# The transposed delta-rule inverse in a hybrid decoder block: 32x32 block transposes on VectorE in place of TensorE turns and ScalarE copies

## What is computed

```python
a_mat = jnp.where(strict, jnp.einsum("bhnid,bhnjd->bhnij", kb, kc) * decay, 0.0)
rhs = jnp.concatenate([vb, kb * jnp.exp(gcum)[..., None]], axis=-1)
sol = lax.linalg.triangular_solve(a_mat + jnp.eye(c, dtype=f32), rhs, left_side=True,
                                  lower=True, unit_diagonal=True)
value, kcd = sol[..., :dv], sol[..., dv:]
```

## Time and profile before

| | |
|---|---|
| median of 3 runs | 565.91 us |
| lowest and highest run | 564.29 and 566.18 us |
| span of the profiled execution | 562.4 us |
| TensorE busy | 556.3 us (99%) |
| VectorE busy | 386.9 us (69%) |
| ScalarE busy | 309.4 us (55%) |
| GpSimd busy | 73.0 us (13%) |
| DMA, mean | 175 GB/s |

### The profile page before, as it was taken

The page is one execution under the profiler, slowest core; times in us unless marked ns, Lnnn a source line. Parts: engine busy times, 40 slices in busy tenths (PEclk is TensorE's granted clock), DMA queues, the critical chain, the costliest instruction groups (busy, mean ns, idle before and its releaser), DMA issues.

```text
span 562.4 us, 9437 instructions
## 1 busy us (share of the span) xinstructions
PE 556.3 (99%) x3695; PEld 482.1 (86%) x3695; DVE 386.9 (69%) x618; ACT 309.4 (55%) x530; POOL 73.0 (13%) x90
## 2 busy tenths in 40 slices
PE   8999999999999999999999999999999999999997
PEld 8999999787787898888888888898888888888885
DVE  6879988858375735898874575666666666757564
ACT  6767668626455656665745434466555545454541
POOL 4221211872610000035000000000000000000000
PEclk9999999999999999999999999999999999999999
DMA  9945576275995461344252556654657666566622
GB/s 300 261 146 175 179 189 225 83 228 198 239 230 178 152 224 32 120 150 147 91 203 84 177 198 196 178 152 151 212 167 217 171 204 194 180 185 191 202 98 75
DMA packets 95323, 98.14 MB, mean 175 GB/s; under 512 B 4986, under 2 KB 75661, under 8 KB 95280
## 3 DMA queue, kind: packets, MB, share of 16 engines
q1 hardware_dynamic: 92992, 93.63, 53.0%
q0 software_dynamic: 2000, 2.87, 2.7%
q10 hardware_dynamic: 288, 1.05, 0.5%
HBM read 96.39 MB, written 1.84 MB: 175 GB/s over the span
## 4 chain that ended last, share of the span: by engine, by line
PE 95%; DVE 3%; ACT 1%; DMA 1%; issue 0%; DVEq 0%; ACTq 0%
PE ps L1537 19%; PE ps L1539 18%; PE ps L1538 18%; PE ps L1653 14%; PE ps L1656 7%; PE ps L1542 4%; PE ps L1776 4%; PE ps L1939 2%; PE ps L1913 2%; PE ps L1628 1%; PE ps L1802 1%; PE ps L1811 1%; DMA x_sb<-in_x 1%; PE ps L1936 1%; DVE out_sb L1530 0%; DVE w_lo L1038 0%
## 5 line engine op out<-in xcount | busy, mean ns | idle before, releaser
L1038 DVE TENSOR_TENSOR w_lo<-raw,w_hi 128x2048 fp32r<-128x2048 f32 x74 | 171.5, 2317 | 96.8 <-ACT w_hi L653 96.7
L653 ACT ACTIVATE w_hi<-raw 128x2048 fp32r<-128x2048 f32 x74 | 141.6, 1913 | 80.5 <-PE ps L1539 71.1
L1653 PE MATMUL ps<-h_both,w_hi 128*128 128x512 f32 x352 | 122.4, 396 | 0.2 <-issue 0.2
L1656 PE MATMUL ps<-h_both,w_lo 128*128 128x256 f32 x352 | 91.1, 279 | 0.3 <-DVE h_both L1064 0.3
L1653 PEld LDWEIGHTS ps<-h_both,w_hi 128*128 128x128 f32 x352 | 63.8, 188 | 13.7 <-issue 2.0
L1656 PEld LDWEIGHTS ps<-h_both,w_lo 128*128 128x128 f32 x352 | 66.3, 188 | 4.0 <-issue 0.6
L1537 PE MATMUL ps<-w_hi,h_both 128*128 128x512 f32 x160 | 65.4, 409 | 0.3 <-DVE zs L1392 0.2
L1539 PE MATMUL ps<-w_hi,h_both 128*128 128x512 f32 x160 | 62.6, 391 | 0.0
L1538 PE MATMUL ps<-w_lo,h_both 128*128 128x512 f32 x160 | 62.4, 390 | 0.0
L1537 PE MATMUL ps<-h_both,w_hi 128*128 128x256 f32 x208 | 59.5, 286 | 0.0
L1538 PE MATMUL ps<-h_both,w_hi 128*128 128x256 f32 x208 | 58.8, 283 | 0.0
(11 more groups left out here) (391 smaller groups left out, 969.3 us busy)
## 6 DMA issues: line engine op xcount, KB each, us to landing
raw<-in_w_in SPq DMA_DIRECT2D x29, 1024.0 KB, 5.1
raw<-in_w_gate SPq DMA_DIRECT2D x22, 512.0 KB, 3.9
raw<-in_w_up SPq DMA_DIRECT2D x22, 512.0 KB, 5.1
raw<-in_w_down SPq DMA_DIRECT2D x11, 1024.0 KB, 4.8
raw<-in_cmp_w SPq DMA_DIRECT2D x8, 1024.0 KB, 5.7
raw<-in_w_proj_a SPq DMA_DIRECT2D x4, 1024.0 KB, 4.9
raw<-in_w_proj_b SPq DMA_DIRECT2D x4, 1024.0 KB, 5.1
raw<-in_w_out SPq DMA_DIRECT2D x4, 1024.0 KB, 5.0
```

Of the source, the lines that this page charges most:

```text
L653: nc.scalar.activation(w_hi[s % NSPL][:], raw[RAW_OF[n]][:], ACT.Copy).then_inc(hi_done, 1)
L1038: nc.vector.tensor_tensor(w_lo[s % NSPL][:], raw[RAW_OF[n]][:], w_hi[s % NSPL][:].bitcast(f32), ALU.subtract).then_inc(lo_done, 1)
L1653: cross = lambda stop: pe.matmul(banks[part][:], hi[:, k, part * P:(part + 1) * P], h_both[:, :, k, :], start=(k == 0), stop=stop)
L1656: end = pe.matmul(banks[part][:, 0:SEQ], lo[:, k, part * P:(part + 1) * P], h_hi[:, k, :], start=False, stop=False)
```

## The change

The stages `T4` and `T5` are taken out of the list of stages, with their places, their TensorE transposes and their ScalarE copies. In their place VectorE transposes blocks of 32x32 elements directly from `Db` into `DTb`, right after its part of `Y4` and `Y5`. After level 4 the four 32x32 diagonal blocks have changed, and four instructions move them; after level 5 the blocks in rows 32 to 63 and 96 to 127 beside them have changed, and two instructions move these. Each instruction has 32 partitions by 16 problems by 32 columns. The new semaphore `inverse_turned` is raised by the last of them; `Y5` waits for its first step, `Z6` for its second.

```diff
-    STAGES += [f"X{_l}"] + ([f"Y{_l}", f"T{_l}"] if _l < LEVELS - 1 else [f"Z{_l}"])
+    STAGES += [f"X{_l}", f"Y{_l}" if _l < LEVELS - 1 else f"Z{_l}"]
...
-            ("cmpv", 0, 0): "X4", ("wv", 0, 0): "Y4", ("wv", 0, 1): "T4", ("cmpv", 1, 0): "X5", ("wv", 1, 0): "Y5", ("wv", 1, 1): "T5",
+            ("cmpv", 0, 0): "X4", ("wv", 0, 0): "Y4", ("cmpv", 1, 0): "X5", ("wv", 1, 0): "Y5",
...
-                    if name == "knT" or name[0] in "XT":
-                        dst = {"k": ATb, "X": AXb, "T": DTb}[name[0]]
+                    if name == "knT" or name[0] == "X":
+                        dst = ATb if name == "knT" else AXb
...
+            def turn_inverse(l):
+
+                for b in range(NB - GRING, NB):
+                    wait_use(dve, f"Y{l}", b)
+                s = 32
+                if l == FIRST_LEVEL:
+                    moves = [(i, i) for i in range(P // s)]
+                else:
+                    moves = [(i + 1, i) for i in range(0, P // s, 2)]
+                for i, o in moves:
+                    ins = nc.vector.transpose(DTb[o * s:o * s + s, :, i * s:i * s + s], Db[i * s:i * s + s, :, o * s:o * s + s])
+                ins.then_inc(inverse_turned, 1)
...
                     for name, blocks in slot_stages(n, half):
                         gdn(name, blocks)
+                        if name[0] == "Y":
+                            turn_inverse(int(name[1:]))
...
-                        if name[0] == "T":
-                            src, before = Db, f"Y{name[1:]}"
...
                         if l > FIRST_LEVEL:
-                            wait_use(pe, f"T{l - 1}", b)
+                            pe.wait_ge(inverse_turned, l - FIRST_LEVEL)
```

More of the change, by code:

```diff
@@ L369, in hybrid_block @@
             "sub_out", "sub_in", "solved", "sub_back", "diag_in"))
+        inverse_turned = sem("inverse_turned")
         small_raw, small_mm = sem("small_raw"), sem("small_mm")
@@ L1780, in gdn @@
                             last = transpose(b4[:, q, :], p4(kT if name == "kt" else vT)[:, q, :])
-                    elif name == "knT" or name[0] == "T":
-                        if name[0] == "T":
-                            src, before = Db, f"Y{name[1:]}"
-                        else:
-                            src, before = AXb, "kt"
-                        wait_use(pe, before, b)
+                    elif name == "knT":
+                        wait_use(pe, "kt", b)
                         for q in range(4):
-                            last = transpose(b4[:, q, :], p4(src)[:, q, :])
+                            last = transpose(b4[:, q, :], p4(AXb)[:, q, :])
                     elif name in ("gram", "kq"):
```

## The result

| | before | changed |
|---|---|---|
| median, us (4 runs each, same chip) | 565.38 | 568.92 |
| lowest and highest, us | 564.29 to 566.18 | 568.41 to 569.36 |
| span of the profiled execution, us | 562.4 | 566.4 |
| granted clock, mean of an execution | 1.00 | 0.997, 0.994, 0.994, 0.994 |

The ratio is 1.0069, 95% interval 1.0053 to 1.0084: slower by 3.5 us by the medians, clear of 0.3%. On another chip the ratio was 1.0065 (1.0052 to 1.0078). No measurable change (566.4 us) had been forecast as the likeliest, at 0.64, and 0.31 given to slower; 568.92 lies just inside the range.

The account below looks back on a forecast made before the run. TensorE was taken to bound the kernel. A wait at the first place (+2.1) and a gain at the second (-1.67) summed to +0.45 us on the 562.4 us span, giving 566.4 us, range 564.8 to 569.0.

Parts of the forecast that it names:

- What bounds the kernel: Whole kernel: TensorE, busy 99% of the span and 95% of the last chain, so work taken from its queue shortens it.
- the 1.78 and 1.77 us on TensorE: At `T4` and `T5`: time of the removed TensorE transposes, 3.55 us gained if nothing else moved.
- The ScalarE copies: Eight copies into `DTb`, 2.07 us for four, go too; counted at nothing.
- The missing cover: `wv` 0: `keys(0)` queues behind four transposes, so TensorE waits some 3.8 us for `key_n`; +2.1 us.
- Rival B: Behind the new 3.8 us stall the clock falls to half rate, adding 1.5 to 3 us; about 568.2 us, chance 0.17.
- the likeliest case: Whole kernel: no measurable change, 566.4 us, second place's gain eaten up by the first's wait; chance 0.60.
- the sum (+0.45): Both places together: +2.1 - 1.67 = +0.45 us on a span of 562.4, so 562.85.
- The second place: `wv` 1, level 5 transposes: TensorE 1.77 us earlier, no wait, 0.1 allowed for what is tight; -1.67 us.
- A: VectorE transposes at the price of scattered operands, 1.08 us row: +2.65, 568.5 us, slower; chance 0.15.
- C: Full saving at both places, `key_n` not late: 3.55 us gained, 562.4 us; chance 0.04.
- D: VectorE's work hidden at both places and TensorE not on the path: time stays at 565.9 us; chance 0.04.
- the lower end: VectorE transpose price from a 512-element MEMSET, 0.48 us: 1.7 us for the four of level 4.

Follow-up runs that it names:

- level 5 only: Against the kernel before: only `T5` goes to two VectorE transposes, `T4` stays on TensorE with its ScalarE copies; 562.70 us, ratio 0.9960.
- the kernel with `keys(0)` first: Against the changed kernel: on VectorE `keys(0)` runs right behind `Y4`, the four level 4 transposes behind it; 563.23 us, 0.9970 of the kernel before.
- the filled kernel: Against the changed kernel: 20 identity matmuls on TensorE ahead of its wait for `key_n`; 566.56 us, 1.0027 of the kernel before.
- the two covered kernels: Against the changed kernel: transposes and `key_tok` turn moved where nothing should wait, 562.97 us (0.9979); then also the query norms' root ahead of `Y4`, 564.79 us (0.9993).

## Why the prediction was wrong

- **What bounds the kernel, and the 1.78 and 1.77 us on TensorE.** Right: `Y5` to the turn of `sc` is 1.78 us shorter, and level 5 only gains 2.2 us. The ScalarE copies cost and gave nothing.
- **The missing cover.** Right in kind: the wait stands at `key_tok`, and the order on VectorE makes it, as the kernel with `keys(0)` first shows. It was undersized: +2.87 us for +2.1. The transposes took 2.85 us for the 2.49 of the nearest row, and began 0.13 behind the last `copy_predicated`, not 0.03; no overlap with the next instruction came back (the sum took off 0.1); and TensorE started 0.15 behind the end of the scaling (170.48 to 170.63), not 0.05.
- **The clock.** This is the step that failed. Rival B described what happened, at its place and with its price (568.2 us), and was given 0.17; the likeliest case had a stall of 3.8 us and no fall. The reason given against it, that no row shows a fall, was no reason: the longest wait in those rows was 1.0 us, so they could not show what one of 3.8 us does. With a wait of 3.8 us the clock falls in 10 runs of 11. With the fall in the likeliest case the forecast would have been rival B's 568.2; measured was +1.57 us for the one fall in the profiled execution. The rule cited beside it, from the Trainium skill (TensorE: Matmul & The Clock Gate, Why this matters for your kernels), that idle gaps between bursts bring the lower clock back, held: behind the 4.5 us the granted clock is 0.50. It is the term that decides between no change and slower: the filled kernel, with the same wait and the clock kept, stands at 1.0027, just within the 0.3% that the prediction called no change. It is not the whole miss. Of the 3.55 us between the sum (+0.45) and the profiled span (+4.0), the clock is 1.57, the longer wait 0.74, `Z6` 0.3, and 0.97 lie outside both places. So that 568.2 comes within 0.7 us of 568.92 is in part luck: rival B too had the shorter wait and nothing for the 0.97.
- **The second place.** Right but for `Z6`: +0.40 us instead of 0.1. The end of the split came at 186.95, against 185.3 for the end of `TURN_LC`, and the logits behind it were later by more than the chain's slack. That the transposes ahead of them did it is shown by the kernel in which they stand behind the logits, where the distance is 8.61 us again.
- **Not in the sum at all:** +0.14 ahead of `Y4` and +0.83 behind the turn of `pc`. The former is within the scatter between executions: `Y4` starts anywhere from 160.2 to 161.4 us in the sixteen traces, with the same matmuls ahead of it. 0.35 of the latter is a pause of TensorE that the profile puts down to "issue". The pause ahead of the SwiGLU matmul is 0.5 us in five of the kernels run and 0.2 in the others, and follows neither the stages that they have nor their order on VectorE; what sets it, and the 0.05 a round, is open.
- **Rivals A, C, D.** A fell: 0.71 us an instruction is nearer to 0.6 than to 1.08. The level of the lower end, 0.41 to 0.48, was not reached either. C and D fell with the wait.

## What to carry to other kernels

Where work moves off the engine that bounds the kernel, ask first what is queued behind it on the engine that receives it, and whether the bounding engine waits for that: the same six instructions cost 3.5 us in one order and gave 1.6 in another. Where a new wait of TensorE appears in the working that is as long as those here (a fall in 9 of 12 runs at 3.0 us, 10 of 11 at 3.8), put the fall of the clock into the likeliest case, not among the rivals; a trace without long gaps is silent on it. Where TensorE is made faster, look also at the transfers: two kernels here outran their weights, and one profiled execution without a fall of the clock could not show why others had one. A wait can be filled, moved or shortened by an experiment, and each shows another part of its price.

## What the runs showed of the hardware

- VectorE's 32x32 block transpose of fp32, 32 partitions by 512 elements: 0.71 us each back to back, against 0.6 for a subtraction of 128 by 512. With a quarter of the partitions it still took longer.
- TensorE's clock falls in some runs of a kernel and not in others, more often the longer the stall: 0 of 10 runs at 1.4 us, 9 of 12 at 3.0, 10 of 11 at 3.8, 14 of 14 at 4.5. A fall lasts some 3.4 us and costs 1.5 to 1.6 us in each of the five traces that have one (1.2 to 2.0 us between whole runs); some runs have a mean clock that means twice as long, which no trace shows.
- It can also fall without a long wait. The one trace of this has it right behind `Z6`, with no wait over 0.41 us in the stages that changed; another execution of the same kernel waited 1.3 us there and kept its clock. It fell in 4 and 8 of 12 runs of the two covered kernels, and what brings it about is open. Moving four transposes of TensorE away from there made the time less steady.
- Fp32 transposes on TensorE, 41 in 4.6 us, kept the clock up in 11 of 11 runs, as 20 matmuls did in 6 of 6.
